# Weighting expert results at eviction and summing them in memory with an accumulating scatter

## The reference

```
h = RMSNorm(x);  z = h @ w_in
x2 = x + (sigmoid(ga) * pool_branch + sigmoid(gb) * retention_branch) @ w_out
h2 = RMSNorm(x2)
for each token: the best of 4 groups, in it the 2 best of 8 experts,
    weight_j = p_group * softmax(top 2)_j
moe(t) = sum over j of weight_j * ( silu(h2 @ w1[e_j]) * (h2 @ w3[e_j]) ) @ w2[e_j]
y = RMSNorm(x2 + moe) * g_final
```

## Time and profile before

| | |
|---|---|
| three runs | 1139.65 us median (1138.45 to 1140.73) |
| the profiled execution | 1142.15 us, span 1140.4 us |
| PE, DVE, ACT, POOL busy | 89%, 70%, 40%, 17% of the span |
| memory read, written | 171.65 MB, 34.45 MB |

### The profile page before, as it was taken

One profiled execution on the slowest core, in us unless ns is written; L12 is line 12 of the kernel. 1 busy time (PEld: TensorE's weight loads), 2 busy tenths in 40 slices (PEclk: granted clock), 3 DMA queues, 4 the chain that ended last, 5 costly groups with the idle time before them and its releaser, 6 DMA issues.

```text
span 1140.4 us, 18415 instructions
## 1 busy us (share of the span) xinstructions
PE 1016.6 (89%) x5408; PEld 867.1 (76%) x5409; DVE 803.1 (70%) x2075; ACT 455.2 (40%) x924; POOL 193.8 (17%) x250
## 2 busy tenths in 40 slices
PE   5799999999999999999988999958999999999920
PEld 5788887888778888788866888747878878787710
DVE  5675566565565556655565666669999999999858
ACT  6411112011120111201112111148889888889732
POOL 0001220012200122001220000021233333233200
PEclk9899999999999999999989999959999999999965
DMA  8511015010150101501036221458999999999556
GB/s 264 179 37 47 15 52 173 10 47 15 53 174 10 48 15 62 165 10 48 15 112 209 113 96 70 157 230 324 348 357 362 367 374 365 358 362 359 207 203 259
DMA packets 73547, 190.28 MB, mean 167 GB/s; under 512 B 12351, under 2 KB 47403, under 8 KB 60011
## 3 DMA queue, kind: packets, MB, share of 16 engines
q1 hardware_dynamic: 61403, 163.88, 39.2%
q0 software_dynamic: 12064, 25.39, 6.1%
HBM read 171.65 MB, written 34.45 MB: 181 GB/s over the span
## 4 chain that ended last, share of the span: by engine, by line
PE 71%; DVE 12%; DMA 7%; issue 5%; ACT 3%; SPq 1%; DVEq 0%; ACTq 0%; POOL 0%; POOLq 0%
PE bank L1729 16%; PE bank L800 9%; PE bank L802 8%; PE bank L801 8%; PE bank L827 8%; PE bank L1730 8%; DMA w<-in_w_dram 3%; ACT w_hi L699 2%; PE bank L856 2%; DVE line L1940 2%; DVE w_lo L1138 2%; PE bank L934 2%; PE bank L1626 1%; PE bank L1618 1%; PE bank L1751 1%
## 5 line engine op out<-in xcount | busy, mean ns | idle before, releaser
L1138 DVE TENSOR_TENSOR w_lo<-w,w_hi 128x512 fp32r<-128x512 f32 x256 | 160.0, 683 | 3.6 <-ACT w_hi L699 3.4
L699 ACT ACTIVATE w_hi<-w 128x512 fp32r<-128x512 f32 x256 | 141.2, 629 | 7.2 <-PE bank L802 4.9
L800 PE MATMUL bank<-w_hi,xT_hi 128*128 128x512 f32 x256 | 104.7, 409 | 17.5 <-DVE xT_lo L1149 12.1
L1729 PE MATMUL bank<-wvg_hi,hT_hi 128*128 128x512 f32 x288 | 117.0, 406 | 0.0
L1579 ACT ACTIVATE v<-bank 128x256 f32<-128x256 f32 x36 | 13.8, 382 | 252.7 <-PE bank L1730 252.7
L1729 PE MATMUL bank<-wvg_lo,hT_hi 128*128 128x512 f32 x288 | 113.5, 394 | 0.0
L1729 PE MATMUL bank<-wvg_hi,hT_lo 128*128 128x512 f32 x288 | 113.2, 393 | 0.0
L800 PE MATMUL bank<-hT_hi,wuqk_hi 128*128 128x344 f32 x288 | 97.3, 338 | 9.2 <-DVE qT L1916 6.9
L802 PE MATMUL bank<-w_hi,xT_lo 128*128 128x512 f32 x256 | 101.7, 397 | 0.0
L801 PE MATMUL bank<-w_lo,xT_hi 128*128 128x512 f32 x256 | 101.4, 396 | 0.0
L801 PE MATMUL bank<-hT_lo,wuqk_hi 128*128 128x344 f32 x288 | 94.1, 327 | 0.0
(11 more groups left out here) (223 smaller groups left out, 2358.1 us busy)
## 6 DMA issues: line engine op xcount, KB each, us to landing
w<-in_w_dram SPq DMA_DIRECT2D x96, 1024.0 KB, 12.8
raw<-in_w_in_dram SPq DMA_DIRECT2D x60, 256.0 KB, 3.3
parts<-part_d SPq DMA_DIRECT2D x8, 1024.0 KB, 11.6
xall<-in_x_prompt_dram SPq DMA_DIRECT2D x8, 512.0 KB, 6.4
mixed_d<-mixed POOLq DMA_DIRECT2D x32, 128.0 KB, 2.1
sample_state<-in_state_ret_dram SPq DMA_DIRECT2D x16, 256.0 KB, 3.7
out_dram<-sample_state SPq DMA_DIRECT2D x16, 256.0 KB, 3.9
mixed_in<-mixed_d SPq DMA_DIRECT2D x8, 512.0 KB, 4.3
```

The lines of the kernel that those rows point to most:

```text
L699: act.activation(hi, whole_w, ACT.Copy).then_inc(S["up_hi"], 1)
L800: pe.matmul(out, lhs[0], rhs[0], start=first, stop=False)
L1138: dve.tensor_tensor(lo, whole_w, hi, ALU.subtract).then_inc(S["up_lo"], 1)
L1729: g = pe.matmul(gates, x[xi], wvg[wi][:, 1:3, k, :], start=first, stop=last)
```

## The change

The weight of each place is put through the same one-hot product as the place's token, as three bf16 parts that sum to it (`weight_planes` on DVE, `weight_list` on PE behind the up-product of expert 0, `slot_weights` on DVE behind the gate of expert 0). `slot_w` then holds for expert b one weight per partition, and ACT evicts the results with it as scale. x2 is written to memory (`sum_d`) by POOL in stage C, and the scatter adds the weighted rows to the token's row of `sum_d`. Since two experts can hold the same token, each scatter now waits until the scatter before it has landed. It uses the gather's index column, kept in six buffers, so the copy of the pair index goes. The last stage loads one row per token into x2's place; `add_parts` is gone, and the groups of the norm are (0,2), (2,5), (5,9). `slot_hot` moves to another place in SBUF, where it lives until `weight_list`.

```diff
-    part_d = nc.dram_tensor("part_d", [2 * NTOK, D], F32).ap()
+    sum_d = nc.dram_tensor("sum_d", [NTOK, D], F32).ap()
...
-        NORM_GROUPS = ((0, 6), (6, 8), (8, 9))
-        TAIL = [("add", n) for n in range(7)] + [("norm", 0)] + [("scale", n) for n in range(3)] \
-            + [("add", 7), ("add", 8), ("norm", 1)] + [("scale", n) for n in (3, 4)] + [("norm", 2)] \
-            + [("scale", n) for n in range(5, 9)]
+        NORM_GROUPS = ((0, 2), (2, 5), (5, 9))
+        TAIL = [step for g, (a, b) in enumerate(NORM_GROUPS)
+                for step in [("norm", g)] + [("scale", n) for n in range(a, b)]]
...
-                sp.dma_start(parts[n][r, :, :].rearrange("p j n -> p (j n)"),
-                             part_d[2 * t * P:2 * (t * P + r.stop), :].rearrange("(p j) n -> p (j n)", j=2))\
-                    .then_inc(rows_in[n], 16)
+                sp.dma_start(x2[r, t, :], sum_d[t * P:t * P + r.stop, :]).then_inc(rows_in[n], 16)
...
             def y_out_of_psum(b, s2):
+                if is_first(b, 1):
+                    act.wait_ge(S["slot_w"], after(1))
                 act.wait_ge(S["down_used"], after(4 * (b + 1)))
                 for n in range(2):
-                    act.activation(yb[s2][:, n * 512:(n + 1) * 512], banks[5 + n][:, :], ACT.Copy)\
-                        .then_inc(S["y_ev"], 1)
+                    act.activation(yb[s2][:, n * 512:(n + 1) * 512], banks[5 + n][:, :], ACT.Identity,
+                                   scale=slot_w[:, bass.ds(b, 1)]).then_inc(S["y_ev"], 1)
...
+            def weight_list():
+                pe.wait_ge(S["hot_done"], after(NT + 1))
+                for i in range(2 * NT):
+                    mm = pe.matmul(banks[7][:, 0:3 * NE], slot_hot[:, i // 2, i % 2, :],
+                                   w_planes[:, i, :, :].rearrange("p a e -> p (a e)"), start=(i == 0),
+                                   stop=(i == 2 * NT - 1))
+                mm.then_inc(S["list_mm"], 1)
...
             def step_m(b, s, g):
                 up(b, s % SLOTS, s % 2)
+                if is_first(b, 1):
+                    weight_list()
...
+            def weight_planes():
+                flat = pair_w[:, :, :].rearrange("p t j -> p (t j)")
+                high, mid, low = (w_split[:, :, i] for i in range(3))
+                b0 = w_bf[:, :]
+                do(dve.tensor_copy(b0, flat))
+                do(dve.tensor_copy(high, b0))
+                do(dve.tensor_tensor(w_rest[:, :], flat, high, ALU.subtract))
+                do(dve.tensor_copy(b0, w_rest[:, :]))
+                do(dve.tensor_copy(mid, b0))
+                do(dve.tensor_tensor(low, w_rest[:, :], mid, ALU.subtract))
+                dve.tensor_tensor(w_planes[:, :, :, :], chosen[:, :, :].unsqueeze(2).to_broadcast([P, 2 * NT, 3, NE]),
+                                  w_split[:, :, :].unsqueeze(3).to_broadcast([P, 2 * NT, 3, NE]), ALU.mult)\
+                    .then_inc(S["hot_done"], 1)
+
+            def slot_weights():
+                dve.wait_ge(S["list_mm"], after(2))
+                dve.tensor_reduce(slot_w[:, 0:NE], banks[7][:, 0:3 * NE].rearrange("p (a e) -> p e a", a=3), AX, ALU.add)\
+                    .then_inc(S["slot_w"], 1)
...
                 gate(b, s % 2)
+                if is_first(b, 1):
+                    slot_weights()
...
-            for k in range(KT):
+            for k in range(4):
+                up_low(0, 0, k)
+            pair_weights()
+            weight_planes()
+            for k in range(4, KT):
                 up_low(0, 0, k)
             x_low(0, 0)
-            pair_weights()
...
                     pool.dma_start(h2_d[t * P:(t + 1) * P, :], h2[s][:, :]).then_inc(h2_out[s], 16)
+                    pool.dma_start(sum_d[t * P:(t + 1) * P, :], x2[:, t, :]).then_inc(x2_out, 16)
...
-            def scatter(b, slot, used, s2):
-                if not is_first(b, SLOTS):
-                    pool.wait_ge(part_out[slot], 16 * (used - 1))
+            def scatter(b, slot, used_by_last, s2, index):
+                if is_first(b, 1):
+                    pool.wait_ge(x2_out, 16 * NT)
+                else:
+                    pool.wait_ge(part_out[(slot - 1) % SLOTS], 16 * used_by_last)
                     carried(pool, "pool")
-                pool.tensor_copy(jcol[slot][:, :], idx_pair[:, bass.ds(b, 1)]).then_inc(S["jcol_done"], 1)
-                pool.wait_ge(S["jcol_done"], after(b + 1))
-                carried(pool, "pool")
                 pool.wait_ge(S["y_ev"], after(2 * b + 2))
                 carried(pool, "pool")
                 pool.indirect_dma_start(
-                    out=part_d, out_offset=bass.IndirectOffsetOnAxis(ap=jcol[slot][:, :], axis=0),
+                    out=sum_d, out_offset=bass.IndirectOffsetOnAxis(ap=index[:, :], axis=0),
                     in_=yb[s2][:, :], in_offset=None,
-                    bounds_check=2 * NTOK - 1, oob_is_err=False).then_inc(part_out[slot], 16)
+                    bounds_check=NTOK - 1, oob_is_err=False, compute_op=ALU.add).then_inc(part_out[slot], 16)
```

More of the change, by code:

```diff
@@ L262, in step_kernel @@
         wr = rc.place("w_router", [P, KT, 36], F32)
+        slot_hot = nc.alloc_sbuf_tensor_at("slot_hot", [P, NT, 2, P], BF16, offset=rc.at)
+        rc.at += NT * 2 * P * 2
         pick_s = rc.place("pick_scratch", [P, 48], F32)
@@ L279, in step_kernel @@
         spill = rc.place("spill", [P, 2 * SPILL + 1], I32)
-        icol = [rc.place(f"icol{i}", [P, 1], I32) for i in range(SLOTS)]
-        jcol = [rc.place(f"jcol{i}", [P, 1], I32) for i in range(SLOTS)]
+        icol = [rc.place(f"icol{i}", [P, 1], I32) for i in range(2 * SLOTS)]
+        slot_w = rc.place("slot_w", [P, NBLK], F32)
+        w_split = rc.place("w_split", [P, 2 * NT, 3], F32)
+        w_rest = rc.place("w_rest", [P, 2 * NT], F32)
+        w_bf = nc.alloc_sbuf_tensor_at("w_bf", [P, 2 * NT], BF16, offset=rc.at)
+        rc.at += -(-2 * NT * 2 // 32) * 32
         chosen = rc.place("chosen", [P, 2 * NT, NE], F32)
@@ L323, in step_kernel @@
         assert rx.at <= rc.where["vec"], (rx.at, rc.where["vec"])
-        rf = Region(nc, at_W, 2 * 3 * KT * (P + DV) * 4)
-        parts = [rf.place(f"parts{i}", [P, 2, D], F32) for i in range(NT)]
+        w_planes = nc.alloc_sbuf_tensor_at("w_planes", [P, 2 * NT, 3, NE], BF16, offset=rx.where["y1"])
         gfin_b = rc.place("gfin_b", [P, D], F32)
@@ L787, in stage_c_act @@
                 r = rows_of(n)
-                act.wait_ge(S["x3_done"], after(n + 1))
+                act.wait_ge(rows_in[n], 48 if n == CH else 32)
                 act.wait_ge(S["sq3_done"], after(n))
@@ L921, in spill_list @@
                 for i in range(2 * NT):
-                    mm = pe.matmul(banks[0][:, 0:3 * SPILL], ov_hot[:, i, :], ov_planes[:, i, :], start=(i == 0),
+                    mm = pe.matmul(banks[0][:, 0:6 * SPILL], ov_hot[:, i, :], ov_planes[:, i, :], start=(i == 0),
                                    stop=(i == 2 * NT - 1))
@@ L1218, in spill_list @@
                                         ALU.mult))
+                for i in range(3):
+                    st.do(dve.tensor_tensor(ov_planes[:, :, (3 + i) * SPILL:(4 + i) * SPILL], hot,
+                                            along(w_split[:, :, i], SPILL), ALU.mult))
                 dve.tensor_tensor(ov_planes[:, :, 2 * SPILL:3 * SPILL], hot, along(misc[:, TILE:TILE + 2 * NT], SPILL),
@@ L1228, in spill_list @@
                 gap, pair = ov_vec[:, 0, 0:SPILL], ov_vec[:, 7, 0:SPILL]
+                st.do(dve.tensor_reduce(slot_w[:, NE:NBLK], banks[0][:, 3 * SPILL:6 * SPILL]
+                                        .rearrange("p (a e) -> p e a", a=3), AX, ALU.add))
                 st.do(dve.tensor_scalar(gap, banks[0][:, 0:SPILL], -4096.0, 4096.0, ALU.mult, ALU.add))
@@ L1266, in stage_c_dve @@
             for kind, n in TAIL:
-                if kind == "add":
-                    add_parts(n)
-                elif kind == "norm":
+                if kind == "norm":
                     a, b = NORM_GROUPS[n]
@@ L1287, in stage_c_pool, with gather @@
             pool.wait_ge(S["routed"], after(1))
-            def gather(b, slot, used):
+            def gather(b, slot, used, index):
                 if not is_first(b, SLOTS):
@@ L1295, in gather @@
                     carried(pool, "pool")
-                pool.tensor_copy(icol[slot][:, :], idx_tok[:, bass.ds(b, 1)]).then_inc(S["icol_done"], 1)
+                pool.tensor_copy(index[:, :], idx_tok[:, bass.ds(b, 1)]).then_inc(S["icol_done"], 1)
                 pool.wait_ge(S["icol_done"], after(b + 1))
@@ L1329, in more @@
                 carried(pool, "pool")
-                gather(b, 0, MAIN_USES[0] + i + 1)
-                scatter(b, 0, MAIN_USES[0] + i + 1, 0)
+                for s in range(SLOTS):
+                    pool.wait_ge(part_out[s], 16 * MAIN_USES[s])
+                gather(b, 0, MAIN_USES[0] + i + 1, icol[0])
```

(1 more changed line is left out.)

27 lines of the change are left out of this document (10 added, 17 removed).

## The result

| | before | after |
|---|---|---|
| median (range, runs) | 1139.84 us (1138.45 to 1140.73, 4) | 1169.29 us (1165.74 to 1172.56, 4) |
| ratio to before | | 1.0236, 95% interval 1.0211 to 1.026 |
| the profiled execution | 1142.15 us, span 1140.4 | 1170.64 us, span 1168.4 |

The kernel became slower by 2.4%, 28 to 29 us. The forecast of 1144 had the direction right; the time is inside the range of 1123 to 1176, but 25 us above the point, in the stretch that was given to "the add is dear". The change forecast was +4.8 us, a sixth of what came: that the time is in the range is due to the range's width and not to the sum.

What follows compares the result with a forecast made beforehand. The prediction saw PE, DVE and DMA engines all nearly full in the expert loop. Last stage -17.0, loop start +3.1 and chained scatter +18.7 gave +4.8 on 1139.65, so 1144 us, range 1123 to 1176.

Steps and rivals of the forecast that it cites:

- the add is dear: Rival in the expert loop: the add lengthens each scatter's landing by 3.9 us, giving 1179 us; chance 0.20.
- Last stage: After the last scatter: adds removed and loads halved, ACT pacing; gain 18.2 us, net -17.0 with the slower last landing.
- The last landing: End of the expert loop: the last, now accumulating scatter lands in its own 3.2 us plus 0.7 to 1.5.
- Start of the loop: Before and behind expert 0's up-product: added DVE and PE weight work, PE starting 2.4 us later; +3.1 us, bounds 0 and 4.0.
- Eviction at nothing: Two ACT evictions per expert, now with per-row scale: up to 0.6 us more each is hidden; zero, barring table loads.
- x2 written to memory: Stage before the expert loop: nine more POOL DMAs, hidden in idle time; zero, at most a microsecond.
- The scatter: Expert loop: the add's second read costs 0.75 us per scatter and each waits for the one before; +18.7 us.
- the chain: Likeliest case, expert loop: scatters waiting on each other's landing set a period of 10.80 us against 10.09; chance 0.45.
- The engines, not the chain: Rival in the expert loop: 10.2 us of DMA work per expert sets the pace, 1129 to 1147 us; chance 0.13.
- The loop hides it: Rival in the expert loop: added read free, 10.05 us fits under 10.09, period kept, 1126 us; chance 0.22.
- The signs: Trace marks: scatters released by DMA, about 0.85 us after a landing; period 10.8; PE waiting for gathers; tail 26 us.

Runs made afterwards that it cites:

- e12: e6 with the two evictions as plain copies, weights left out of the results: 1126.11 us, ratio 0.9872, period 10.09 us.
- e1: The changed kernel with the scatter as a plain write, still waiting for the scatter before, sums left out: 1127.45 us, ratio 0.987.
- e3: e2 with the scatter as a plain write, so neither add nor wait for the scatter before; sums left out: 1127.95 us, ratio 0.987.
- e2: The changed kernel, still adding, with experts ordered across the groups and no wait for the scatter just before: 1160.89 us, ratio 1.016.
- e5: The changed kernel with places dealt to partitions in bit-reversed order, so live rows spread over all partitions: 1136.05 us, ratio 0.9937.
- e6: e2 with the bit-reversed places of e5, so adding, without the wait, rows spread: 1129.36 us, ratio 0.9907.
- e9: The changed kernel with places dealt in turn to the two halves of the partitions, in order within each half: 1147.22 us, ratio 1.0035.
- e10: The changed kernel with places bit-reversed only inside each half of 64 partitions, live rows staying in the first half: 1163.48 us, ratio 1.0199.
- e11: e6 with the scatter as a plain write, sums left out: 1129.94 us, ratio 0.9906.
- e4: The changed kernel, still adding and waiting for the scatter before, with only the expert order across groups of e2: 1167.73 us, ratio 1.0224.
- e7: The kernel before with only the bit-reversed places: 1138.5 us, ratio 0.9987.
- e8: e3 with one more gather of the same h2 rows behind each scatter, into a buffer nobody reads: 1171.0 us, ratio 1.0244.

## Why the prediction was right and wrong

*Last stage, right.* -18.2 were worked out for the stretch behind the last landing and -17.0 measured. ACT paces it as foreseen, but with small gaps where a load came late:

```profile
1146.47 1.06 ACT L793 ACTIVATE junk_f<-x 128x1024 f32<-128x1024 f32 x1 [0.90 <-DMA x<-sum_d]
...
1150.08 1.06 ACT L793 ACTIVATE junk_f<-x 128x1024 f32<-128x1024 f32 x1 [1.09 <-DMA x<-sum_d]
...
1156.38 1.06 ACT L793 ACTIVATE junk_f<-x 128x1024 f32<-128x1024 f32 x1 [1.28 <-DMA x<-sum_d]
...
1158.87 0.30 ACT L347 ACTIVATE small<-small 128x4 f32<-128x4 f32 x1
...
1160.08 5.00 DVE L1296 SCALAR_TENSOR_TENSOR x<-x,small,gfin_b 128x1024 f32<-128x1024 f32 x5
```

ACT started its first 128-row tile at 1146.47, 3.9 us behind the last landing (4.0 were foreseen), and the last root came at 1158.87, 12.4 us later where 11.0 were worked out. ACT waited 1.09 and 1.28 us for two of the loads: they pace it too, and that is the missing microsecond. The last landing was mis-sized: 6.0 us against the 3.9 to 4.7 allowed.

*Start of the loop, the steps right, the sum too high.* The large product took what was worked out (1.98 us against 1.9), and the first up-product started late:

```profile
758.25 1.98 DVE L1156 TENSOR_TENSOR w_planes<-chosen,w_split 128x1728 bf16<-128x1728 f32 x1
...
763.34 0.77 PE L803 MATMUL bank<-w_hi,xT_hi 128*128 128x512 f32 x1 [2.53 <-issue]
...
770.29 0.94 PE L972 MATMUL bank<-w_planes,slot_hot 128*128 128x96 bf16 x18
...
771.71 0.25 DVE L1162 TENSOR_REDUCE slot_w<-bank 128x32 f32<-128x96 f32 x1
```

Yet the first scatter started 0.7 us earlier than before. Stage C ended 0.9 us earlier in this execution, and relative to that the scatter is only 0.2 us late: the experts that follow caught the 2.4 us up, which was the lower bound of that step, and should have been its value.

*Eviction at nothing: wrong by some 3.5 us.* "Up to 0.6 us more for each is hidden": 0.09 us each were not (e12). The table load that was named as the exception didn't come.

*x2 written to memory: right.* With the plain write the whole change comes to 0.987 (e1, e3), within a microsecond or two of what the last stage gives less the eviction; no room is left there for a cost of the nine writes.

*The scatter: the step that failed.* The prediction said: "a scatter is half of the 1.47 us above, and a second pass over its rows doubles it", and then "I take 0.75", put on the landing of a chain that sets the pace. The work was right: +0.72 us on the mean of 16 engines, 10.2 us per expert. Two things in it were wrong. The 0.75 is a mean, and nearly all rows lie in half of the partitions, so the engines that carry them get about twice that (an estimate from where the rows lie, 2 x 0.72 = 1.4 us), on top of what already fell on them alone. The loop then waits for the fullest ones: in e2 for weights, in the kernel after for gathers. That the place of the rows is the cause is shown (e5, e6, e9, e10, e11); the factor of two is not. And the chain isn't the cause of the period but follows it: taken away (e2), it gives back 7 to 8 us of the loss by the medians, and taken alone (e1, e3) it costs nothing. The measured +42.2 us of the loop divide so: by periods, e3 against before +3.4 (the eviction, 28 x 0.12), e2 against e3 +27 (the add on uneven engines, 28 x 0.97), after against e2 +12 (chain and order, 28 x 0.42, in these two profiled executions; e4's 11.38 makes it 6).

*The rivals.* "The engines, not the chain" was right in kind, and its sign was right: without the chain, ACT waits for weights. It had 0.13 because its price was taken at the mean share that before reached, 0.94, and so came to 10.86 at most; measured 11.18. "The loop hides it" at 1126 is what the kernel does when the add is gone or spread (e1, e6). "The add is dear" had the time nearly right, for a reason that the runs don't bear out: it put 3.9 us on the landing of a chain, while the landing grew by 1.3 us in the loop (mean of 28, 9.1 to 10.4) and by 2.8 alone at the end, and e2 keeps most of the loss with no chain.

*The signs.* Nearly every sign that the prediction named for the chain was in the trace of after, and the chain was still not the main cause. The two that were off, the size of the period and the 6.0 us of a scatter with nothing beside it, were the ones to follow. A scatter that waits for the one before it shows its landing time, whatever made the landing long; the signs told how the delay travels, not where it starts. Another cause of long landings would have shown the same.

What stays open: the load of each engine was not seen, only inferred from where the rows lie and from the number of packets under way; how the add lengthens a lone landing even with spread rows (4.8 us in e5, by the first load that waits for it, against 2.7 in e7); and the chain's small cost with spread rows (e5 against e6) is at the edge of what the runs tell apart.

## What to carry to other kernels

A mean DMA share over 16 engines says little when transfers skip rows: ask which partitions the live rows lie in, and if they fill from one end, deal them over all partitions (here one constant, 3.0 points of the kernel after). A kernel can be at that edge with hardly a wait that shows it, and then the next bit of traffic costs more than its mean: here 0.97 us of period for 0.72 us of mean engine time. Where accumulating transfers must not overlap, order the work so that those that conflict are far apart, in place of waiting for each. And before a wait is called the cause, take it away in a kernel and look whether the period falls.

## What the runs showed of the hardware

- Moving the same rows to other partitions changed the kernel by 3.0 points (after 1.0236, e5 0.9937) and let the mean DMA share in the loop rise from 0.88 to 0.99.
- A scatter that adds cost the engines about what a plain read of the same rows does: +0.72 us per expert (e2 against e3) and +0.74 (e8 against e3). With the rows spread it cost no time (0.9907 against 0.9906).
- Alone at the end, an accumulating scatter landed after 6.0 us where the plain one took 3.2; with the rows spread, after 4.8 (e5, by the first load that waits for it) against 2.7 (e7). Issuing one takes POOL 1.6 us (median of e2) to 2.1 (e6), where the plain one takes 1.5.
- With the rows in the first places at most 12 packets were under way in 27% of the loop's stretch (after), with the rows spread in 3% (e5).
- A per-row scale adds 0.09 us to an eviction of 128 x 512 on ACT (683 against 597 ns). The Trainium skill (ScalarE: Activation LUTs, What ACT_TABLE_LOAD costs) gives about 93 ns for each pointer operand; by that page, the trace agrees.
